# A two-layer hybrid backbone on one core: layer 1's input projection split in three and pipelined by tile, queries and keys projected in turns, values behind the first scores

## The chip, the cores and the metric

One core of one Trainium2 chip. The metric is the device time of one execution in microseconds (us); the kernel before has a median of 1917.29 us over three runs (1916.35 to 1918.03).

## What is computed

A stream of 512 latent and 256 context rows of 1024 features goes through two layers. Layer 0 mixes by a gated linear recurrence, layer 1 by attention; each is followed by a mixture of 16 experts, whose weights (12 MB each) are streamed from HBM. The change lies in layer 1's mixer:

```python
def mla_qkv(h, w_in, q_norm, kv_norm, w_uq, w_ukv, cos, sin):
    z = h @ w_in                                   # 1024 -> 384 + 256 + 32
    cq, ckv, kr = z[..., :384], z[..., 384:640], z[..., 640:]
    q = (rmsnorm(cq, q_norm) @ w_uq).reshape(B, L, 16, 96)
    kv = (rmsnorm(ckv, kv_norm) @ w_ukv).reshape(B, L, 16, 64 + 64)
    # q's last 32 and kr are rotated for latent rows (apply_rope);
    # k = 64 of kv beside kr, the same for all heads; v = the other 64
def attend(q, k, v):
    s = einsum('bqhd,bkhd->bhqk', q, k) * 96 ** -0.5
    return einsum('bhqk,bkhd->bqhd', softmax(s), v)
```

512 latent rows are queries; keys and values come from all 768 rows.

## The kernel before, in words

Everything is written out by hand for five engines, which meet at semaphores only. Rows are worked in tiles of 128: TLT = 4 latent tiles, TT = 6 tiles in all. An F32 tensor that has to go through TensorE faster is kept as a high part of type F32R (a copy by ACT, `hi`) and the rest (a subtraction by DVE, `lo`), and a product is then three matmuls: hi x hi, lo x hi, hi x lo. The scores (L935, L936), layer 0's input projection (L590) and both output projections (L650) do this; layer 1's input projection (L845, L846) and the projections of queries (L899) and of keys and values (L880) are F32 matmuls.

**Input projection of layer 1** (PE L845 and L846, in the loop over `step`). After layer 0's experts the stream is read back into `x_b`. For all six tiles ACT squares and sums (`squares`, L998, L999), DVE scales (`normed_tile`, L1283, L1284), PE turns the tile (`turn_tile`, L516 into `turned`), ACT and DVE modulate half of it each (`modulate`, L1008 and L1292) into `hT2`. ACT and DVE do this in `norm(2)`, for six tiles, before anything else. PE projects tile 0, turns tile 2, projects tile 1, turns tiles 3, 4 and 5, and goes on; a latent tile gets 672 columns, a context tile only the last 288. Behind each projection ACT squares the latent (L1228 to L1232), DVE scales it into `cqn` (L1659 to L1663), copies 32 columns to `kraw` and rotates them into `krr` (L1645, L1670), PE turns `cqn` (L516 into `duo`), and DVE writes `cqT` and `ckvT` (L1678, L1681). PE turns tile t's only when DVE has done the `cqT` of t - 1.

**The attention loop** (`Fori` over NG = 4 groups of HG = 4 heads). A projection stage: six times keys and values (`kv_project`, 512 columns, `duo` bank t % 2), each copied by DVE into `ktok` and `V` (L1699 to L1701), turned by PE (`turn_keys`), copied by ACT to `k_hi` (L1237) and subtracted by DVE to `k_lo` (L1706); then four times queries (`q_project`, 384 columns) with a rotation on DVE (L1718, L1645, L1722), turned, `q_hi` (L1242), `q_lo` (L1728). `turned` has one bank for keys and one for queries, so a turning waits for the low part of the one before. A score stage: 16 units u of one head and one query tile. PE computes scores (`scores`, L935, L936, banks 2 * (u % 2) of `wide`), DVE the maximum (L1745), ACT the exponential (L1259), DVE the reciprocal (L1741), POOL scales (L1877), PE turns the probabilities LAG = 3 units later (L516 into `turned`), ACT and DVE copy them to `PT` (L1251, L1753), and every second unit PE multiplies by the values (`values`, L958) into `duo`.

**Around it.** The output projection (`residual_norm` on DVE, L1455 and L1461 for the low parts of weight blocks and rows) is followed by the choice of rows and the experts. DVE opens the ring's other slots for the experts' weights in `choose`; SP's queue issues every weight load in one fixed order (L463), and four of its slots open at the end of the attention loop.

Of the kernel before, what the change touches and what calls it, by code (L numbers as in the profile page):

```python
# [15 lines left out]
ALU = mybir.AluOpType  # L16
# [6 lines left out]
P = 128  # L23
# [21 lines left out]
def build(nc, x, c, ctx, c_ctx, ada_w, ada_b, norm_mix, norm_ffn, norm_final, lru_w_in, lru_conv_w, lru_conv_b,  # L45
# [143 lines left out]
    with ExitStack() as es:  # L189
# [71 lines left out]
        def flat(a, n, w):  # L261
# [8 lines left out]
        sub, (xn2, hT2, cqn, kraw) = phase(("xn2", [P, TT, D], F32), ("hT2", [P, KD, T], F32),  # L270
                                           ("cqn", [P, 2, QL + KVL], F32), ("kraw", [P, 2, ROPE], F32))
# [64 lines left out]
            "s_S", "s_max", "s_exp", "s_pn", "s_ptr", "s_PTd", "s_PTa", "s_av", "s_OT", "s_rs")]  # L336
        s_fin, s_out, s_nf = sem("s_fin"), sem("s_out"), sem("s_nf")
# [60 lines left out]
        W0 = [2 * KD, 3 * KD]  # L398
        L0 = [KD, KD + TT]
# [104 lines left out]
        def _(pe):  # L504
# [315 lines left out]
            hT = stages[2]["hT"]  # L820
            for j in range(3):
                arrived(("mla_in", j))

            def mla_w(k):
                j = [n for n, (a, b) in enumerate(MLA_K) if a <= k < b][0]
                return ring_at(("mla_in", j))[:, (k - MLA_K[j][0]) * MZ:(k - MLA_K[j][0] + 1) * MZ]

            for step in range(TT + 1):
                if step < TT:
                    t = step  # L830
                    if t >= 2:

                        pe.wait_ge(s_cqn, t - 1)
                    else:

                        pe.wait_ge(s_ye[0], E + 1)
                        pe.wait_ge(s_modcol, 6)

                    pe.wait_ge(s_hTa, N0[2] + t + 1)
                    pe.wait_ge(s_hTd, N0[2] + t + 1)  # L840
                    b = 2 * (t % 2)
                    for k in range(KD):
                        lhs = hT[:, k, t * P:(t + 1) * P]
# [27 lines left out]
            with pe.Fori(0, NG) as g:  # L871

                def kv_project(t):


                    if t < 2:
                        pe.wait_ge(s_OT, g * 2 + (t + 1))
                    pe.wait_ge(s_ktok, g * 6 + (t + 1))
                    for k in range(KKV):
                        ins = mm(duo[:, t % 2, :], ckvT[:, k, t * P:(t + 1) * P],  # L880
                                 ring_at(("ukv", k))[:, bass.ds(g * BANK, BANK)], start=k == 0, stop=k == KKV - 1)
                    ins.then_inc(s_kv, 1)
# [10 lines left out]
                def q_project(t):  # L893

                    if t < 2:
                        pe.wait_ge(s_ktok, g * 6 + (t + 7))
                    pe.wait_ge(s_qtok, g * 4 + (t + 1))
                    for k in range(KQ):
                        ins = mm(duo[:, t % 2, 0:HG * QK], cqT[:, k, t * P:(t + 1) * P],  # L899
# [11 lines left out]
                kv_project(0)  # L911
                for t in range(1, TT):
                    kv_project(t)
                    turn_keys(t - 1)
                q_project(0)
                turn_keys(TT - 1)
                for t in range(1, TLT):
                    q_project(t)
                    turn_queries(t - 1)
                turn_queries(TLT - 1)  # L920
# [61 lines left out]
        def _(act):  # L982
# [28 lines left out]

            def norm(s):
                n = stages[s]["n"]
                for step in range(n + 1):
                    if step < n:
                        squares(s, step)
                    if step >= 1:
                        modulate(s, step - 1)
# [200 lines left out]
            norm(2)  # L1219

            for t in range(TT):
# [10 lines left out]
                fn(mx[:, 3, t:t + 1], mx[:, 1, t:t + 1], ACT.Sqrt, bias=eps[:, 0:1], scale=1.0 / KVL).then_inc(s_mzs, 1)  # L1232
            with act.Fori(0, NG) as g:
                for t in range(TT):
                    act.wait_ge(s_ktr, g * 6 + (t + 1))

                    fn(k_hi[:, :, t * P:(t + 1) * P], turned[0:QK, 1, :].rearrange("p (h n) -> p h n", h=HG),  # L1237
                       ACT.Copy).then_inc(s_khi, 1)
                for t in range(TLT):
# [31 lines left out]
        def _(dve):  # L1271
# [23 lines left out]

            def norm(s):
                n = stages[s]["n"]
                for step in range(n + 1):
                    if step < n:
                        normed_tile(s, step)  # L1300
                    if step >= 1:
                        modulate(s, step - 1)
# [331 lines left out]
            norm(2)  # L1634

            def turn_angles(dst, src, n, t):

                x1 = src.rearrange("p n (a h f) -> p n a h f", a=2, h=2)[:, :, :, 0, :]
                x2 = src.rearrange("p n (a h f) -> p n a h f", a=2, h=2)[:, :, :, 1, :]
                o1 = dst.rearrange("p n (a h f) -> p n a h f", a=2, h=2)[:, :, :, 0, :]  # L1640
                o2 = dst.rearrange("p n (a h f) -> p n a h f", a=2, h=2)[:, :, :, 1, :]
                cos, sin = [ropes[:, t, i, :].rearrange("p (a f) -> p a f", a=2).unsqueeze(1).to_broadcast([P, n, 2, FQ]) for i in range(2)]
                tmp = [rtmp[:, j, 0:n * 2 * FQ].rearrange("p (n a f) -> p n a f", n=n, a=2) for j in range(4)]
                for j, (a_, b_) in enumerate(((x1, cos), (x2, sin), (x1, sin), (x2, cos))):
                    ins = v.tensor_tensor(tmp[j], a_, b_, ALU.mult)  # L1645
                return ins, [(o1, tmp[0], tmp[1], ALU.subtract), (o2, tmp[2], tmp[3], ALU.add)]


            dve.wait_ge(s_rope, 16)
            for step in range(TT + 1):  # L1650
                if step < TT:
# [13 lines left out]
                    if t < TLT:  # L1665
                        chain.step(v.tensor_copy(kraw[:, t % 2, :], kr))
                        ins, rest = turn_angles(krr[:, t:t + 1, :], kraw[:, t % 2:t % 2 + 1, :], 1, t)
                        chain.step(ins)
                        for o, a_, b_, op in rest:
                            ins = v.tensor_tensor(o, a_, b_, op)  # L1670
                        ins.then_inc(s_cqn, 1)
# [236 lines left out]
```

## Time and profile before

| | us |
|---|---|
| median of three runs | 1917.29 |
| the profiled execution | 1916.38 |
| its span, first to last instruction | 1914.6 |
| PE busy | 1655.4 (86%) |
| DVE busy | 653.2 (34%) |
| ACT busy | 514.2 (27%) |
| POOL busy | 202.5 (11%) |
| mean DMA rate over the span | 276 GB/s |

PE busy counts a matmul from its start to a modelled end. The profiled execution's time has 1.8 us around its span. The chain of work that ended last is PE for 61% of the span, SP's queue for 20%.

### The profile page before, as it was taken

How to read it: one execution, taken by the hardware profiler on the slowest of the kernel's cores; microseconds unless marked ns; L12 is line 12 of the kernel's file. 1: busy time of each engine (PE TensorE's matmuls, PEld its weight loads, DVE VectorE, ACT ScalarE, POOL GpSimd, SP SyncE). 2: the span in 40 equal slices, each digit the busy share in tenths (PEclk: the TensorE clock that was granted, in tenths of full speed). 3: DMA queues.
4: the chain of work that ended last, by engine and by line, in shares of the span. 5: the costliest groups of instructions: out<-in, count | busy, mean ns of one | idle time of the engine just before them, and what ended most of it. 6: DMA issues, size and time to landing. Idle time of an engine off the chain costs nothing.

```text
span 1914.6 us, 22850 instructions
## 1 busy us (share of the span) xinstructions
PE 1655.4 (86%) x9277; PEld 816.8 (43%) x9277; DVE 653.2 (34%) x1359; ACT 514.2 (27%) x873; POOL 202.5 (11%) x199
## 2 busy tenths in 40 slices
PE   5999969579999999999879989988849978777874
PEld 2677748323333333333245757757613322222221
DVE  4666664611212212122234655655441101011111
ACT  5678763201101111011141534535300000000001
POOL 1000010000000000000000413413000100000000
PEclk8999989789999999999979899899969999999998
DMA  9454441899999999998741000002589999999997
GB/s 364 165 199 157 176 176 78 338 374 409 410 396 403 404 390 406 382 403 322 254 169 66 1 0 0 0 0 119 209 338 405 398 398 414 400 413 398 412 408 290
DMA packets 92084, 528.61 MB, mean 276 GB/s; under 512 B 11875, under 2 KB 20176, under 8 KB 36448
## 3 DMA queue, kind: packets, MB, share of 16 engines
q1 hardware_dynamic: 80704, 489.84, 63.6%
q0 software_dynamic: 11296, 37.58, 6.9%
q8 instruction: 62, 1.02, 0.2%
q14 instruction: 22, 0.18, 0.0%
HBM read 504.21 MB, written 23.17 MB: 275 GB/s over the span
## 4 chain that ended last, share of the span: by engine, by line
PE 61%; SPq 20%; ACT 6%; DVE 5%; DMA 5%; issue 3%; ACTq 0%; DVEq 0%; POOLq 0%
SPq L463 20%; PE wide L737 14%; PE duo L777 6%; PE wide L650 6%; PE wide L745 6%; PE turned L516 6%; PE wide L590 5%; PE duo L787 3%; PE duo L958 2%; PE wide L935 2%; PE duo L880 2%; DMA sb_ring<-ada_w 2%; DMA sb_ring_x<-moe_w_down 1%; PE duo L899 1%; PE wide L845 1%
## 5 line engine op out<-in xcount | busy, mean ns | idle before, releaser
L737 PE MATMUL wide<-sb_ring_x,sb_xT 128*64 128x512 f32 x1136 | 271.5, 623 | 33.6 <-DMA sb_ring_x<-moe_w_up 32.5
L737 PE MATMUL wide<-sb_ring,sb_xT 128*64 128x512 f32 x912 | 212.3, 607 | 29.1 <-DMA sb_ring<-moe_w_up 27.4
L1565 DVE TENSOR_TENSOR sb_hid<-wide,sb_sg 128x512 f32<-128x512 f32 x32 | 22.1, 692 | 616.6 <-ACT sb_sg L1174 310.9
L1174 ACT ACTIVATE sb_sg<-wide 128x512 f32<-128x512 f32 x32 | 19.2, 599 | 668.2 <-PE wide L745 340.8
L737 PEld LDWEIGHTS wide<-sb_ring_x,sb_xT 128*64 128x64 f32 x1136 | 79.0, 142 | 212.6 <-issue 140.5
L777 PE MATMUL duo<-sb_ring_x,sb_hidT 128*64 128x512 f32 x592 | 138.3, 600 | 10.3 <-DMA sb_ring_x<-moe_w_down 10.1
L1865 POOL DMA_INDIRECT stream<-sb_ye,sb_idx_t x30 | 43.1, 1435 | 901.6 <-DVE sb_ye L1588 901.6
L737 PEld LDWEIGHTS wide<-sb_ring,sb_xT 128*64 128x64 f32 x912 | 62.1, 138 | 166.0 <-issue 108.4
L1877 POOL TENSOR_TENSOR sb_prob<-sb_prob,sb_asum 128x768 f32<-128x768 f32 x64 | 93.9, 1467 | 261.3 <-DVE sb_asum L1741 261.3
L1580 DVE SCALAR_TENSOR_TENSOR sb_ye<-duo,sb_gate_t,sb_gffn 64x512 f32<-64x512 f32 x30 | 22.3, 742 | 203.9 <-PE duo L787 103.6
L1194 ACT ACTIVATE sb_ye<-duo 64x512 f32<-64x512 f32 x30 | 17.9, 596 | 271.1 <-PE duo L787 146.8
L777 PE MATMUL duo<-sb_ring,sb_hidT 128*64 128x512 f32 x368 | 86.1, 600 | 4.9 <-DMA sb_ring<-moe_w_down 4.4
L777 PEld LDWEIGHTS duo<-sb_ring_x,sb_hidT 128*64 128x64 f32 x592 | 38.1, 136 | 97.0 <-issue 67.3
L590 PE MATMUL wide<-sb_hT_hi,sb_w_hi 128*128 128x512 f32 (+1 forms) x256 | 70.2, 355 | 7.7 <-DVE sb_hT_lo L1387 7.7
L1259 ACT ACTIVATE sb_prob<-wide,sb_asum 128x768 f32<-128x768 f32 x64 | 57.9, 904 | 31.6 <-DVE sb_asum L1745 31.6
L590 PE MATMUL wide<-sb_hT_lo,sb_w_hi 128*128 128x512 f32 (+1 forms) x256 | 66.0, 339 | 0.0
L590 PE MATMUL wide<-sb_hT_hi,sb_w_lo 128*128 128x512 f32 (+1 forms) x256 | 65.9, 338 | 0.0
L745 PE MATMUL wide<-sb_ring_x,sb_xT 128*32 128x512 f32 x568 | 65.6, 595 | 0.0
L1745 DVE TENSOR_REDUCE sb_asum<-wide 128x1 f32<-128x768 f32 x64 | 60.7, 948 | 13.2 <-PE wide L936 13.0
L516 PE MATMUL turned<-sb_ident,sb_prob 128*128 128x128 f32 x384 | 54.2, 278 | 5.1 <-ACT sb_PT L1251 5.1
L745 PE MATMUL wide<-sb_ring,sb_xT 128*32 128x512 f32 x456 | 52.7, 595 | 0.0
L1251 ACT ACTIVATE sb_PT<-turned 128x512 f32<-128x512 f32 x64 | 38.1, 596 | 41.8 <-PE turned L516 40.4
(336 smaller groups left out, 2517.4 us busy)
## 6 DMA issues: line engine op xcount, KB each, us to landing
sb_ring_x<-moe_w_up SPq DMA_DIRECT2D x142, 1024.0 KB, 15.0
sb_ring<-moe_w_up SPq DMA_DIRECT2D x114, 1024.0 KB, 18.9
sb_ring_x<-moe_w_down SPq DMA_DIRECT2D x80, 1024.0 KB, 18.0
sb_ring<-moe_w_down SPq DMA_DIRECT2D x48, 1024.0 KB, 16.1
sb_ring<-ada_w SPq DMA_DIRECT2D x40, 1024.0 KB, 6.8
sb_ring<-lru_w_in SPq DMA_DIRECT2D x8, 1024.0 KB, 9.1
sb_ring_x<-ada_w SPq DMA_DIRECT2D x8, 1024.0 KB, 7.5
sb_ring<-lru_w_out SPq DMA_DIRECT2D x4, 1024.0 KB, 6.6
```

Of the source, the lines that this page charges most:

```text
L463: sp.dma_start(dst, src).then_inc(landed[slot], 16)
L516: return nc.tensor.transpose(dst, src, ident[0:n, 0:n])
L590: ins = mm(wide[:, b, :] if i == 0 else wide[:, b + 1, 0:TC], w[:, p % 2, k, :], seg(h[:, k, :], i), start=k == 0 and n == 0, stop=k == KD ...
L650: ins = mm(wide[:, b + n, :], lhs[:, k, :], w[:, n * BANK:(n + 1) * BANK], start=k == 0 and i == 0, stop=k == KD - 1 and i == 2)
L737: ins = mm(wide[n * CAPL:(n + 1) * CAPL, s, :], xT[:, k, 0:CAPL], w[:, at:at + BANK], start=k == 0, stop=k == KD - 1)
L745: ins = mm(wide[n * CAPC:(n + 1) * CAPC, 2, :], xT[:, k, CAPL:M], w[:, n * BANK:(n + 1) * BANK], start=k == 0, stop=k == KD - 1)
L777: ins = mm(lat[n * CAPL:(n + 1) * CAPL, :], hidT[:, 2 * (c % 2) + r, h * CAPL:(h + 1) * CAPL], w[:, r, n * BANK:(n + 1) * BANK], start=c = ...
L787: ins = mm(both[at:at + CAPC, :], hidT_c[:, 2 * (c % 2) + r, h * CAPC:(h + 1) * CAPC], w[:, r, n * BANK:(n + 1) * BANK], start=c == 0, sto ...
L1259: fn(prob[:, u % LAG, :], wide[:, b:b + 2, :].rearrange("p a n -> p (a n)")[:, 0:T], ACT.Exp, bias=asum[:, 0, u % 4:u % 4 + 1], accum_out= ...
L1745: v.tensor_reduce(asum[:, 0, u % 4:u % 4 + 1], wide[:, b:b + 2, :].rearrange("p a n -> p (a n)")[:, 0:T], AX_X, ALU.max, negate=True).then ...
L1865: pool.indirect_dma_start(out=stream, out_offset=bass.IndirectOffsetOnAxis(ap=idx_t[0:M, e:e + 1], axis=0), in_=(ye if e < E - 1 else xg)[ ...
L1877: g_.tensor_tensor(prob[:, u % LAG, :], prob[:, u % LAG, :], asum[:, 2, u % 4:u % 4 + 1].to_broadcast([P, T]), ALU.mult).then_inc(s_pn, 1)
```

## The change

It does four things. (1) Layer 1's input projection becomes three F32R products: ACT copies the eight weight blocks into a new buffer `mla_hi` and each modulated tile into `hT2_hi` (the place of `xn2`), DVE subtracts, in place. (2) The six tiles are pipelined: ACT and DVE prepare three tiles, then one further behind each projection; PE turns tile t + 2 behind projection t. The rotation of `krr` moves from DVE to POOL. (3) In the attention loop queries and keys are projected in turns (`PROJECT`), keys without values (256 columns); the values' projection (256 columns) stands behind the scores of units 0 to 5, with a copy by DVE into `V`; the first multiplication by values waits for all six. (4) In `residual_norm` of both layers DVE subtracts one weight block before the first rows, not two.

```diff
+        sub, (hT2_hi, hT2_lo) = phase(("hT2_hi", [P, TT, D], F32R), ("hT2_lo", [P, KD, T], F32R))
...
+                                                   ("mla_hi", [P, KD, MZ], F32R))
...
+        PROJECT = [("q", 0), ("k", 0), ("q", 1), ("k", 1), ("q", 2), ("k", 2), ("q", 3), ("k", 3), ("k", 4), ("k", 5)]
+        bank_of = {item: i % 2 for i, item in enumerate(PROJECT)}
...
@@ tensor engine, input projection
-                    pe.wait_ge(s_hTa, N0[2] + t + 1)
-                    pe.wait_ge(s_hTd, N0[2] + t + 1)
+                    pe.wait_ge(s_hlo, MLA_L0 + t + 1)
...
-                        if t < TLT:
-                            mm(wide[:, b, 0:QL], lhs, mla_w(k)[:, 0:QL], start=k == 0, stop=k == KD - 1)
-                        ins = mm(wide[:, b + 1, 0:MZ - QL], lhs, mla_w(k)[:, QL:MZ], start=k == 0, stop=k == KD - 1)
+                        if t == 0:
+
+                            pe.wait_ge(s_wlo, MLA_W0 + k + 1)
+                        _, w_hi, w_lo = mla_w(k)
+                        for i, (lhs, w) in enumerate(((lhs_hi, w_hi), (lhs_lo, w_hi), (lhs_hi, w_lo))):
+                            edge = dict(start=k == 0 and i == 0, stop=k == KD - 1 and i == 2)
+                            if t < TLT:
+                                mm(wide[:, b, 0:QL], lhs[:, k, :], w[:, 0:QL], **edge)
+                            ins = mm(wide[:, b + 1, 0:MZ - QL], lhs[:, k, :], w[:, QL:MZ], **edge)
...
-                    for t in {0: (2,), 1: range(3, TT)}.get(step, ()):
-                        turn_tile(2, t)
+                    if step + 2 < TT:
+                        turn_tile(2, step + 2)
@@ tensor engine, loop
+                def v_project(t):
+
+                    if t >= 2:
+
+                        pe.wait_ge(s_V, g * 6 + (t - 1))
+                    for k in range(KKV):
...
+                    ins.then_inc(s_vp, 1)
...
+                for i in range(len(PROJECT) + 1):
+                    if i < len(PROJECT):
+                        what, t = PROJECT[i]
...
+                    if i >= 1:
+                        what, t = PROJECT[i - 1]
+                        if what == "q":
+                            turn_queries(t)
+                        else:
+                            turn_keys(t)
                 pe.wait_ge(s_kT, g * 6 + 7)
...
+                    if w == 0:
+                        pe.wait_ge(s_V, g * 6 + 6)
...
                         scores(u)
+                    if u < TT:
+                        v_project(u)
@@ scalar engine
+            def mla_rows(t):
+
+                modulate(2, t)
+                h, hi, _ = mla_lhs(t)
+                act.wait_ge(s_hTa, N0[2] + t + 1)
+                act.wait_ge(s_hTd, N0[2] + t + 1)
+                fn(hi, h, ACT.Copy).then_inc(s_hhi, 1)
+
+            for t in range(3):
+                squares(2, t)
+                if t >= 1:
+                    mla_rows(t - 1)
...
+                if t + 3 < TT:
+                    squares(2, t + 3)
+                if t + 2 < TT:
+                    mla_rows(t + 2)
@@ vector engine
-                out_weights_lo(lay, 0, 1)
+                out_weights_lo(lay, 0)
                 out_lhs_lo(lay, 0)
-                out_weights_lo(lay, *range(2, KD))
+                out_weights_lo(lay, *range(1, KD))
...
+            def mla_rows(t):
+
+                modulate(2, t)
+                h, hi, lo = mla_lhs(t)
+                dve.wait_ge(s_hhi, MLA_L0 + t + 1)
+                v.tensor_tensor(lo, h, hi.bitcast(F32), ALU.subtract).then_inc(s_hlo, 1)
...
+                        v.tensor_copy(kraw[:, t % 2, :], kr).then_inc(s_cqn, 1)
...
+                    if t + 3 < TT:
+                        normed_tile(2, t + 3)
+                    if t + 2 < TT:
+                        mla_rows(t + 2)
                 if step >= 1:
                     t = step - 1
                     dve.wait_ge(s_cqtr, t + 1)
...
+                    if u < TT:
+
+                        dve.wait_ge(s_vp, g * 6 + (u + 1))
+                        v.tensor_copy(V[:, u, :, :], duo[:, u % 2, 0:HG * VD].rearrange(
+                            "p (h n) -> p h n", h=HG)).then_inc(s_V, 1)
@@ gpsimd
+            for t in range(TLT):
+                pool.wait_ge(s_cqn, t + 1)
+                if t >= 1:
+
+                    pool.wait_ge(s_krr, 6 * t)
+                _, rest = turn_angles(g_, krr[:, t:t + 1, :], kraw[:, t % 2:t % 2 + 1, :], 1, t, s_krr)
+                pool.wait_ge(s_krr, 6 * t + 4)
+                for o, a_, b_, op in rest:
+                    g_.tensor_tensor(o, a_, b_, op).then_inc(s_krr, 1)
```

## Rows read from the trace of the kernel before

**Rows 1.** stretches by stage; window (us), length, busy per engine (instructions), clock, DMA share, GB/s
```profile
967.37:978.98 11.61, 11.61 (x42) 7.90 (x42) 2.89 (x7) 2.58 (x8) 0.00 (x0) 0.85 0.89 347
978.98:988.13 9.15, 9.15 (x36) 6.14 (x35) 2.28 (x6) 2.72 (x7) 0.00 (x0) 1.00 0.00 0
988.13:1000.40 12.27, 4.77 (x31) 3.88 (x30) 8.25 (x30) 8.40 (x27) 0.00 (x0) 0.77 0.00 1
1035.05:1062.14 27.09, 24.61 (x89) 13.20 (x89) 16.48 (x55) 5.35 (x9) 0.00 (x0) 0.94 0.13 51
1062.14:1109.17 47.03, 45.59 (x387) 39.28 (x384) 24.09 (x50) 26.82 (x50) 23.46 (x16) 0.89 0.00 1
1109.17:1134.56 25.39, 22.91 (x90) 12.61 (x89) 17.16 (x56) 5.35 (x9) 0.00 (x0) 1.00 0.00 0
1134.56:1180.26 45.70, 41.97 (x387) 35.75 (x385) 23.66 (x50) 26.60 (x50) 23.47 (x16) 1.00 0.00 0
1400.00:1900.00 500.00, 398.89 (x1732) 125.18 (x1732) 64.27 (x137) 28.70 (x48) 38.28 (x33) 0.95 0.99 392
```

**Rows 2.** timeline of DVE, score stage of the loop's second iteration; start, length, group
```profile
1142.28 0.16 DVE L1741 RECIPROCAL sb_asum<-sb_asum 128x1 f32<-128x1 f32 x1 [1.06 <-ACT sb_prob L1259]
...
1144.44 0.16 DVE L1741 RECIPROCAL sb_asum<-sb_asum 128x1 f32<-128x1 f32 x1 [0.81 <-ACT sb_prob L1259]
```

**Rows 3.** instructions of one line: ns min/median/max, first and last start, shape
```profile
L1135 ACT ACTIVATE sb_OT_hi<-sb_OT x4: 1042/1061/1064, 1324.7 to 1352.3; 128x1024 fp32r<-128x1024 f32 x4
...
L1461 DVE TENSOR_TENSOR sb_OT_lo<-sb_OT,sb_OT_hi x4: 1217/1218/1221, 1326.9 to 1354.7; 128x1024 fp32r<-128x1024 f32 x4
```

**Rows 4.** timeline of PE, scores at full clock (PEld is a weight load)
```profile
1075.98 0.39 PE L935 MATMUL wide<-sb_k_lo,sb_q_hi 96*128 96x512 f32 x1
...
1076.21 0.28 PE L936 MATMUL wide<-sb_k_lo,sb_q_hi 96*128 96x256 f32 x1
...
1076.33 0.40 PE L935 MATMUL wide<-sb_k_hi,sb_q_lo 96*128 96x512 f32 x1
1076.33 0.19 PEld L936 LDWEIGHTS wide<-sb_k_hi,sb_q_lo 96*128 96x128 f32 x1
...
1076.69 0.82 PE L516 MATMUL turned<-sb_ident,sb_prob 128*128 128x128 f32 x6
```

**Rows 5.** timeline of PE, input projection
```profile
988.13 1.04 PE L516 MATMUL turned<-sb_ident,sb_xn 128*128 128x128 f32 x8
...
1026.97 4.05 PE L846 MATMUL wide<-sb_ring,sb_hT 128*128 128x288 f32 x16
```

**Rows 6.** timeline of DVE and ACT, one modulation and the work behind one projection
```profile
994.66 1.37 DVE L1292 TENSOR_SCALAR sb_hT<-turned,sb_cols 128x128 f32<-128x128 f32 x4 [0.75 <-PE turned L516]
...
1021.33 0.49 ACT L1228 ACTIVATE sb_cqn<-wide 128x384 f32<-128x384 f32 x1 [8.12 <-PE wide L846]
...
1022.83 0.16 DVE L1659 RECIPROCAL sb_lam<-sb_mx 128x1 f32<-128x1 f32 x1 [6.17 <-ACT sb_mx L1232]
...
1024.02 0.18 DVE L1666 COPY sb_kraw<-wide 128x32 f32<-128x32 f32 x1
...
1025.65 0.60 DVE L1681 TENSOR_SCALAR sb_ckvT<-duo,sb_pB 128x128 f32<-128x128 f32 x2
```

**Rows 7.** timeline, queries in the projection stage of the loop's second iteration
```profile
1129.38 0.60 PE L516 MATMUL turned<-sb_ident,sb_qtok 128*96 128x128 f32 x4
...
1129.81 2.10 PE L899 MATMUL duo<-sb_ring,sb_cqT 128*128 x6
...
1132.11 0.42 DVE L1718 COPY sb_qtok<-duo 128x256 f32<-128x256 f32 x1 [0.44 <-PE duo L899]
...
1132.47 0.59 ACT L1242 ACTIVATE sb_q_hi<-turned 96x512 fp32r<-96x512 f32 x1 [1.86 <-PE turned L516]
...
1133.37 0.68 DVE L1728 SCALAR_TENSOR_TENSOR sb_q_lo<-turned,sb_q_hi 96x512 fp32r<-96x512 f32 x1
```

**Rows 8.** timeline of PE, start of layer 1's output projection
```profile
1328.23 0.70 PE L650 MATMUL wide<-sb_wo_a,sb_OT_hi 128*128 128x512 f32 x2 [3.17 <-DVE sb_OT_lo L1461]
```

More of the change, by code:

```diff
@@ L819, in _ @@
             turn_tile(2, 1)
[L820 to L826, printed above, removed]
             for step in range(TT + 1):
@@ L909, in turn_queries @@
                     ins.then_inc(s_qtr, 1)
[L911 to L920, printed above, removed]
+                for i in range(len(PROJECT) + 1):
+                    if i < len(PROJECT):
+                        what, t = PROJECT[i]
+                        if what == "q":
+                            q_project(t)
+                        else:
+                            k_project(t)
+                    if i >= 1:
+                        what, t = PROJECT[i - 1]
+                        if what == "q":
+                            turn_queries(t)
+                        else:
+                            turn_keys(t)
                 pe.wait_ge(s_kT, g * 6 + 7)
@@ L1010, in modulate @@
                 ins.then_inc(s_hTa, 1)
[L1012 to L1018, printed above, removed]
             act.wait_ge(s_const, NCONST)
@@ L1218, in _ @@
             act.wait_ge(s_modev, 6)
-            norm(2)
+            for k in range(KD):
+                w, hi, _ = mla_w(k)
+                slot, n, _ = place["mla_in", [j for j, (a, b) in enumerate(MLA_K) if a <= k < b][0]]
+                act.wait_ge(landed[slot], 16 * n)
+                fn(hi, w, ACT.Copy).then_inc(s_whi, 1)
+            def mla_rows(t):
[8 more added lines that the diff above has]
+                    mla_rows(t - 1)
             for t in range(TT):
@@ L1232, in _ @@
                 fn(mx[:, 3, t:t + 1], mx[:, 1, t:t + 1], ACT.Sqrt, bias=eps[:, 0:1], scale=1.0 / KVL).then_inc(s_mzs, 1)
+                if t + 3 < TT:
+                    squares(2, t + 3)
+                if t + 2 < TT:
+                    mla_rows(t + 2)
             with act.Fori(0, NG) as g:
[L1234 to L1239, printed above, removed]
+                for what, t in PROJECT:
+                    if what == "k":
+                        act.wait_ge(s_ktr, g * 6 + (t + 1))
+                        fn(k_hi[:, :, t * P:(t + 1) * P], turned[0:QK, 1, :].rearrange("p (h n) -> p h n", h=HG),
+                           ACT.Copy).then_inc(s_khi, 1)
+                        continue
                     act.wait_ge(s_qtr, g * 4 + (t + 1))
@@ L1294, in modulate @@
                 ins.then_inc(s_hTd, 1)
[L1296 to L1302, printed above, removed]
             def ada_read(i):
@@ L1632, in _ @@
             mod_columns(5)
[L1634 to L1649, printed above, removed]
+            for k in range(KD):
+                w, hi, lo = mla_w(k)
+                dve.wait_ge(s_whi, MLA_W0 + k + 1)
+                v.tensor_tensor(lo, w, hi.bitcast(F32), ALU.subtract).then_inc(s_wlo, 1)
+            def mla_rows(t):
[3 more added lines that the diff above has]
+                v.tensor_tensor(lo, h, hi.bitcast(F32), ALU.subtract).then_inc(s_hlo, 1)
+            for t in range(3):
+                normed_tile(2, t)
+                if t >= 1:
+                    mla_rows(t - 1)
             for step in range(TT + 1):
@@ new lines, in _ @@
+                for i in range(len(PROJECT) + 1):
+                    if i < len(PROJECT):
+                        what, t = PROJECT[i]
+                        if what == "q":
+                            q_tile(t)
+                        else:
+                            k_tile(t)
+                    if i >= 1:
+                        what, t = PROJECT[i - 1]
+                        if what == "q":
+                            q_rest(t)
+                        else:
+                            k_rest(t)
```

134 lines of the change are left out of this document (79 added, 55 removed).

## The prediction

> **What bounds the kernel now.** I read the stretches by stage first, since the change touches one passage: layer 1's input projection (967.4 to 1035.0 us) and the attention loop of four iterations (1035.0 to 1323.8 us). After it, 500 us have the DMA engines 0.99 busy at 392 GB/s [rows 1]: the experts' weights stream, and the stream opens only when the attention is over, so what the attention gives back moves the end one for one; nothing in the stream itself changes.
>
> The PE timeline shows two things in the input projection. A latent tile costs PE 9.15 us, in F32. And between the second and the third tile lie 12.27 us in which PE is busy 4.77 and its granted clock falls to 0.77 of full [rows 1]: PE turns tiles 2 to 5 one after another, each behind ACT's and DVE's modulation, and then waits for the first normalized latent, because ACT and DVE do all six normalizations before they look at the first projection.
>
> In the loop a projection stage takes 25.39 us, 22.91 of it with PE busy, and a score stage 45.70 us at full clock. In the first iteration they took 27.09 and 47.03, at granted clocks of 0.94 and 0.89 [rows 1]; the third iteration repeats the 47.03. In the score stage's first units PE is not the bound: reciprocal follows reciprocal by 2.16 us [rows 2], DVE's maximum and ACT's exponential taking turns.
>
> **The input projection.** *Start, +1.5 us.* The first matmul now needs a copy (1.06) and a subtraction (1.22) of the 1024-wide tile [rows 3] behind the modulation; 0.8 of it lies beside PE's turning of the second tile, so I take 1.5: 968.85 for 967.37. The eight weight copies on ACT and subtractions on DVE (two thirds as wide, so 0.7 and 0.8 us each, 6 us per engine) fit between the end of layer 0's experts and the arrival of the stream rows, where both engines wait; were that cover gone they would cost up to 6.
>
> *A tile, 7.45 us.* Three F32R products take the place of one F32 product. At full clock 512 columns pass in 0.23 us and 256 in 0.12, each with a weight load of its own beside it [rows 4]; 384 and 288 then take 0.175 and 0.135, and 24 such pairs 7.45 us, for 9.15. A context tile is 24 x 0.135 = 3.25, for 3.9 [rows 5]. Bounds: 7.2 if the loads cost nothing, and, with the 0.19 us of a load's record [rows 4] added to each matmul, 16.5. I stay near the low end because the 256-column row already has a load in its 0.12.
>
> *Order.* In series on PE from 968.85: four latent tiles 29.8, 1.5 for the first one's half clock (the first tile took 1.45 longer than the second [rows 1, 5]), four turned tiles of 1.04 [rows 5], three turned latents of 0.6, one context tile 3.25: 1009.4. DVE and ACT need some 9.2 us per tile (squares and roots 1.5, normalization 1.35, cqT 1.4, modulation 1.37 [rows 6], copy, subtraction), against PE's 9.1, with two tiles of lead: they keep up, just. **What is late next** is DVE's FIFO at the end: the sum for tile 5 stands ahead of cqT(2), and PE's fourth turning needs cqT(2). Projection 3 ends near 1004.5; 1.5 + 1.35 + 1.37 + 1.06 + 1.22 + 1.4 and the handings-over put cqT(2) at 1012.6, so PE waits 3 us. Then 0.6, the last tile 3.25, and the tail as before (4.2 us from the last projection to the loop): the loop begins at 1020.8 instead of 1035.05. **-14.2 us.** The rotation of krr leaves DVE (0.65 us per tile off it) for POOL, which has nothing else then; POOL has no row of such small operations, so from 0.2 to 1.5 us each, six a tile: at most 9 us against 9 us per tile, and DVE waits for it only two tiles later and before the loop.
>
> **The loop, projection stage.** Walked with the rows: q takes PE 1.94 and a turning 0.43; the copy starts 0.36 after the projection, DVE's q tile takes 1.26, ACT's copy 0.59, the subtraction 0.68 [rows 7]. Keys alone are 512 columns in place of 1024, so 0.88 by the ratio to q's 1152. In turns, a pair costs q 1.94 + 0.2 + DVE 1.3 + turning 0.43 + handing over = 3.93: k's projection and turning hide inside DVE's 1.3, PE waits 0.6. First turning at 3.5, fourth at 15.3. Then keys 3, 4 and 5 are bound by their chain (turning 0.43, ACT 0.59, DVE 0.69, three handings-over: 2.04 each), and now the scores wait for the last key's low part, which the queries used to cover: scores at 22.7. The same walk of the old order gives 25.2 (measured 25.39 [rows 1]). **-2.5 each.**
>
> **Score stage.** Six projections of values, 0.88 each, come onto PE, and six copies (0.42) onto DVE. Units 0 to 2 have no probabilities to turn: 1.06 (three pairs [rows 4]) + 0.88 fits in 2.16, so they cost nothing while that 2.16 stands. In units 3 to 5 PE has 1.06 + 0.88 + 0.70 for the six turnings [rows 4] = 2.64 for 2.16: +0.48 three times. The copies lie beside ACT's exponential. POOL queue and SP queue issue nothing new. **+1.5 each**, so an iteration is 1.0 shorter, **-4.0** for four.
>
> **The clock.** Before, passages at half clock (1.2 for 2.4 GHz) cost 1.7 at the loop's start and 1.33 in two of four score stages (47.03 for 45.70 [rows 1]), 4.4 in all; the granted 0.89 over 47.03 makes each of the two some 10 us long. The new tail has PE busy 0.9 of 4.8 us ahead of every score stage. The place to compare is ahead of the loop, where PE rested 4.2 us but for a short turning and then ran its first matmuls slow [rows 1, 5]; so I expect a short half-clock passage in all four, and now it hurts more, for the values fill the slack: about 1.6 each, plus 1.3 at the start: 7.7, **+3.3**. Bounds: no fall at all (-4.4), and 10 us of half clock each time, which by the same walk costs 5.1 each, **+17.3**.
> The Trainium skill (TensorE: Matmul & The Clock Gate, Part 1) says that the throttled state is the default and that activity releases it; the fall before the loop agrees, and by it busier first units should end the passage sooner.
>
> **Both output projections.** DVE subtracts weight block 0, then the first rows, then block 1. PE waited 3.17 us for the rows' low part [rows 8]; block 1's subtraction, of the same shape as the rows' (1.22 [rows 3]), stood in it; layer 0 has the same pattern. **-1.1 twice**; block 1 arrives before PE has done block 0's six matmuls.
>
> **Sum**: -14.2 - 4.0 + 3.3 - 2.2 = -17.1. The profiled execution took 1916.38 us, 0.9 under the median of 1917.29; so 1899.3 against it and **1900.2** as a median.
>
> **Rivals.**
> 1. *Long half-clock passages.* 10 us in every score stage: -20.4 + 17.3 = -3.1, 1914; in half of them, 1907. For it: two of four were that long before [rows 1]. Against: PE then had slack, and will not.
> 2. *No falls*: -20.4 - 4.4 + 1.3 = -23.5, 1893.8. For it: iterations two and four had none.
> 3. *F32R pays less.* A tile at 8.3 and 4.0 gives back 4 us: 1904 to 1905; at F32's own time 8 us, 1908.
> 4. *Slower: the weight loads stand in line.* The input projection goes from 80 matmul-and-load pairs to 240. If each new load cost PE 0.087 us or more that nothing hides, the 17.1 and the 3.8 that make a difference are eaten; at the record's 0.19 it is +45.6 less 17.1: 1946. Against it: a 256-column product with its load passes in 0.12 [rows 4].
> The Trainium skill (TensorE: Matmul & The Clock Gate, "LDWEIGHTS" and "Back-to-back issue gap") gives a load columns/1.2 ns, 107 ns for 128, and a spacing set by load and product together; added whole, my estimate from it is 240 x 0.107 = +25.7, 1925.9. The 0.12 us row speaks against taking it whole.
> 5. *Nothing to gain*: the idle 12.27 us only moves, because DVE's FIFO makes PE wait at every tile instead of once. DVE and PE are within 0.1 us per tile; if each of the four steps waited 3 us, -5: 1912.
>
> **How the numbers follow.** Forecast case 0.57, long passages 0.15, no falls 0.12, F32R dearer 0.08, waits at each tile 0.05, slower 0.03. 0.2% is 3.8 us, about what a measurement of this kernel can tell from no change. Cases 1 (all four long) and 5 reach into it with about 0.04. The range goes from 1892 (no falls, tile at 7.2) to 1909 (half of the passages long, or F32R without gain); above it lie all-long, every-tile waits and slower, 0.1 together.
>
> **What would show it.** First loop matmul near 1021 with a latent tile near 7.5 us and no stall over 1.5 us before the last two tiles; one wait of about 3 us ahead of the fourth turned latent. Loop iterations of 70 to 73 us, projection stages of 22.7 with the last wait on k_lo, score stages of 47 to 49 with granted clock below 1.00 in their first 4 us. PE's first output matmul waiting 2 us for OT_lo, not 3.2. Wrong if projection stages are over 24 us, or if a stage after 1300 us changes its length by more than 2 us.

## The result, and the profile of the changed kernel

The changed kernel has a median of 1910.56 us over seven runs (1905.94 to 1915.26), the kernel before 1917.44 beside it (1916.35 to 1919.11): a ratio of 0.9967, with a 95% interval from 0.9954 to 0.9980. A second set of twelve runs gave 0.9970 (0.9958 to 0.9982). So it is faster by 0.3%, some 6 us, where 17 were forecast: 1910.56 lies above the predicted range of 1892 to 1909. The profiled execution took 1912.11 us (its span 1910.4), for a forecast of 1899.3.

First the stretches of the changed kernel (window, length, busy time of each engine with its instructions, granted clock, share and rate of the DMA engines), to be laid beside [rows 1]:

```profile
969.93:980.62 10.69, 10.69 (x56) 10.69 (x57) 3.31 (x7) 2.90 (x8) 0.00 (x0) 0.75 0.82 327
980.62:989.43 8.81, 8.81 (x64) 8.81 (x63) 4.75 (x12) 5.73 (x17) 1.65 (x6) 1.00 0.00 1
...
1024.36:1050.34 25.98, 21.48 (x89) 13.89 (x89) 14.72 (x50) 5.93 (x10) 0.00 (x0) 0.89 0.12 46
1050.34:1099.04 48.70, 47.42 (x408) 41.32 (x408) 25.27 (x55) 26.07 (x49) 23.48 (x16) 0.96 0.01 1
1099.04:1123.00 23.96, 18.74 (x90) 12.51 (x89) 15.32 (x51) 5.93 (x10) 0.00 (x0) 0.98 0.00 0
1123.00:1172.83 49.83, 48.55 (x408) 42.24 (x409) 25.30 (x55) 26.06 (x49) 23.48 (x16) 0.94 0.00 0
1172.83:1196.79 23.96, 18.74 (x91) 12.51 (x89) 15.33 (x51) 5.93 (x10) 0.00 (x0) 1.00 0.00 0
1196.79:1245.51 48.72, 47.44 (x409) 41.31 (x409) 25.18 (x55) 26.07 (x49) 23.48 (x16) 0.96 0.00 0
1245.51:1269.46 23.95, 18.74 (x90) 12.51 (x89) 15.33 (x51) 5.93 (x10) 0.00 (x0) 0.99 0.00 0
1269.46:1319.44 49.98, 48.70 (x408) 42.35 (x408) 25.41 (x55) 26.67 (x50) 23.48 (x16) 0.94 0.00 0
```

Two things are to be seen. The loop begins at 1024.36 where it began at 1035.05, so the input projection gave what it was made for. But the loop takes 295.1 us where it took 288.7: its projection stages are shorter (23.96 for 25.39), its score stages longer (48.7 to 50.0 for 45.7 to 47.0), and the clock is under 1.00 in all four score stages. So 10.7 us are won ahead of the loop and 6.4 given back in it.

Where the input projection ends, the timeline of PE in the changed kernel (start, length, group, idle time before it and what ended that):

```profile
1013.91 1.30 PE L551 MATMUL duo<-sb_ident,sb_cqn 128*128 128x128 f32 x5 [3.42 <-DVE sb_ckvT L1743]
...
1015.24 0.44 PE L878 MATMUL wide<-sb_mla_hi,sb_hT_lo 128*128 128x288 f32 x1
1015.48 0.44 PE L878 MATMUL wide<-sb_ring_r,sb_hT_hi 128*128 128x288 f32 x1
...
1019.76 0.29 PE L878 MATMUL wide<-sb_ring_r,sb_hT_hi 128*128 128x288 f32 x1
1019.89 0.29 PE L878 MATMUL wide<-sb_mla_hi,sb_hT_hi 128*128 128x288 f32 x1
...
1024.36 1.00 PE L945 MATMUL duo<-sb_ring,sb_cqT 128*128 x1 [1.19 <-DVE sb_marks L1345]
```

The forecast wait for cqT(2) is there, 3.42 us of it. Behind it the matmuls of the last tile start 0.24 us apart, and 0.13 apart from 1019.76 on: two levels of the clock, read off the starts.

A stretch of the second iteration's projection stage, PE and DVE, in the changed kernel:

```profile
1102.84 0.64 PE L551 MATMUL turned<-sb_ident,sb_qtok 128*96 128x128 f32 x4 [0.73 <-DVE sb_qtok L1776]
...
1105.26 0.60 PE L551 MATMUL turned<-sb_ident,sb_ktok 128*96 128x128 f32 x4
1105.54 0.42 DVE L1772 COPY sb_qtok<-duo 128x256 f32<-128x256 f32 x1 [0.71 <-PE duo L945]
...
1106.53 0.36 DVE L1776 TENSOR_TENSOR sb_qtok<-sb_rtmp 128x64 f32<-128x64 f32 x2
...
1107.02 0.64 PE L551 MATMUL turned<-sb_ident,sb_qtok 128*96 128x128 f32 x4 [0.30 <-DVE sb_qtok L1776]
...
1118.80 0.61 PE L551 MATMUL turned<-sb_ident,sb_ktok 128*96 128x128 f32 x4 [0.63 <-DVE sb_k_lo L1782]
...
1120.91 0.61 PE L551 MATMUL turned<-sb_ident,sb_ktok 128*96 128x128 f32 x4 [1.49 <-DVE sb_k_lo L1782]
...
1123.00 0.79 PE L984 MATMUL wide<-sb_k_hi,sb_q_hi 96*128 96x512 f32 x1 [1.48 <-DVE sb_k_lo L1782]
```

A pair of query and key takes 4.18 us from turning to turning. Then the last three keys go one behind another, 2.1 us each, and PE rests 0.63, 1.49 and 1.48 us between short turnings. The first score product behind that takes 0.79 us; the same product has 0.48 at full clock (keys_then_queries, in the last section). At the loop's end the output projection waits as forecast, 2.08 us, 1.1 less than in [rows 8]:

```profile
1322.83 0.70 PE L685 MATMUL wide<-sb_wo_a,sb_OT_hi 128*128 128x512 f32 x2 [2.08 <-DVE sb_OT_lo L1520]
```

### The profile page after: what moved, and what is told of

Read it like the earlier page. It is cut to its first block and busy times, and to the rows that moved or that the text cites. A ratio compares the mean times of both kernels' runs of the same rounds, so it can differ in the third digit from the quotient of the medians.

```text
span 1910.4 us, 23222 instructions
## 1 busy us (share of the span) xinstructions
PE 1649.8 (86%) x9453; PEld 843.8 (44%) x9453; DVE 662.3 (35%) x1349; ACT 524.7 (27%) x887; POOL 208.7 (11%) x223
## 3 DMA queue, kind: packets, MB, share of 16 engines
q8 instruction: 63, 1.03, 0.2%
```

## The experiments

All times are medians, each with its ratio to the kernel before run on the same chip. The theory after the result: the loop half of the change loses by itself, because turning in series leaves the last keys' chain bare, and because PE's rest ahead of the scores lets the clock fall.

### The two halves apart

*input_only* has parts (1), (2) and (4) of the change with the old loop; *loop_only* has part (3) with everything else as before. The cut shows one place of input_only's edit.

```diff
 # input_only: PE, ACT and DVE in the loop as before
-                for i in range(len(PROJECT) + 1):
...
+                kv_project(0)
+                for t in range(1, TT):
+                    kv_project(t)
+                    turn_keys(t - 1)
```

> The changed input projection and output order with the old attention loop. Theory (the loop is what lost: its projection stages gain 1.4 us each, its score stages lose 3 us each, half of that to a clock that falls ahead of each): the loop begins near 1024.4 as in the changed kernel, takes some 288.7 us as before, and the time is 11 to 14 us under the kernel before, 1903 to 1906. Rival (the loop is neutral and the 13 us won in the input projection are lost again behind the loop, at the expert weights): the same 1910 as the whole change.

> The old input projection and output order with the changed attention loop. Theory: the loop takes 294 to 296 us where it took 288.7, so the kernel is 5 to 7 us slower than the kernel before, 1922 to 1924. The prediction's own sum had the loop shorter by 0.7 us in all: 1916 to 1917. Rival (the loop's loss comes only from its earlier start or from what the new input projection leaves behind, such as the rotated columns): no slower than the kernel before.

Measured: input_only 1905.00 (0.9940, 0.9927 to 0.9953), its loop beginning at 1021.77 and taking 288.7 us; loop_only 1924.56 (1.0039, 1.0025 to 1.0053), 0.6 above its range. The second iteration of loop_only:

```profile
1111.27:1135.23 23.96, 18.74 (x91) 12.52 (x89) 15.32 (x51) 5.93 (x10) 0.00 (x0) 1.00 0.00 0
1135.23:1183.95 48.72, 47.44 (x408) 41.28 (x408) 25.18 (x55) 26.07 (x49) 23.47 (x16) 0.96 0.00 0
```

They equal the third iteration of the whole change, and the loop as a whole takes 294.5 us for its 295.1: the loop's loss has nothing to do with what stands ahead of it. The halves add up: -0.60% and +0.39%, together -0.21% for -0.33% and -0.30% measured, within the intervals. Nothing that could be told from the scatter was lost behind the loop; the change is a gain of some 12 us and a loss of some 7.

### The clock

*fill* puts useless products where PE rests; *fill_last*, made later, keeps the one directly ahead of the scores.

```diff
+                def fill():
+                    pe.wait_ge(s_ktok, g * 6 + 7)
+                    for k in range(KKV):
+                        ...
+                        mm(duo[:, 0, 0:HG * VD], ckvT[:, k, 0:P], w, start=k == 0, stop=k == KKV - 1)
...
                         else:
+                            if t >= 4:          # fill only
+                                fill()
                             turn_keys(t)
+                fill()
                 pe.wait_ge(s_kT, g * 6 + 7)
```

> The changed kernel with useless products of two matmuls each (256 columns, F32, the shape of the values' projection) at three places where PE waits for the last keys: ahead of the turnings of keys 4 and 5 and ahead of the scores. PE does the same work otherwise. Theory (PE's rest ahead of the scores lets the clock fall, and the fall costs some 2 us a score stage): granted clock 0.99 or more in all score stages, score stages 46.5 to 47.5 instead of 48.7 to 50.0, projection stages within 0.5 us of 23.96, and the time 5 to 9 us under the changed kernel, 1902 to 1906. Rival (the clock is a bystander, the score stages are long because the values' projections collide with units 3 to 5): score stages stay at 48.5 or more, time 1910 or more.

> The changed kernel with the useless product at one of the three places only, directly ahead of the scores; the rests ahead of the turnings of keys 4 and 5 stay. Theory A (what counts is PE's rest directly ahead of the scores): score stages near 47.2 at granted clock 1.00 as with all three, time 1900 to 1904. Theory B (it is the whole tail, some 4.8 us in which PE does little, that lets the clock fall): the fall stays in at least two of four score stages, 47.9 to 50, time 1904 to 1911.

Measured: fill 1901.38 (0.9908, 0.9893 to 0.9922; 0.6 under its range), fill_last 1901.21 (0.9915, 0.9898 to 0.9932). The second iteration of fill, then of fill_last:

```profile
1096.34:1120.41 24.07, 21.21 (x102) 14.60 (x101) 15.32 (x51) 5.92 (x10) 0.00 (x0) 1.00 0.00 0
1120.41:1167.61 47.20, 45.92 (x409) 40.18 (x409) 25.08 (x55) 26.05 (x49) 23.46 (x16) 1.00 0.00 0
```
```profile
1096.22:1120.19 23.97, 19.61 (x95) 13.18 (x93) 15.33 (x51) 5.93 (x10) 0.00 (x0) 1.00 0.00 0
1120.19:1167.29 47.10, 45.82 (x409) 40.08 (x409) 25.11 (x55) 26.07 (x49) 23.48 (x16) 1.00 0.00 0
```

PE does more work and the kernel is 9 us faster (11.6 between fill_last and the changed kernel on one chip; in the profiles fill's loop takes 8 us less). In fill the score stages are at full clock, 47.1 to 47.2 us in all four iterations, so a fall cost 1.5 us in the first and third and 2.6 to 2.8 in the second and fourth. The 47.2 is also the clean price of the values' projections: 1.5 over the 45.70 of [rows 1]. One product directly ahead of the scores gives nearly what three give, but not all of it. In the third iteration of fill_last the clock fell once more, before that product: the turning behind the rest of 1.50 us took 1.06 us instead of 0.61, the product 1.91 instead of 1.03. The cost was 0.4 us in the projection stage and 0.2 to 0.3 in the scores. The third iteration's two stages, then the product in the second iteration beside the third's:

```profile
1167.29:1191.70 24.41, 20.67 (x95) 13.98 (x93) 15.32 (x51) 5.93 (x10) 0.00 (x0) 0.94 0.00 0
1191.70:1239.09 47.39, 46.11 (x410) 40.31 (x409) 25.11 (x55) 26.07 (x49) 23.48 (x16) 0.99 0.00 0
```
```profile
1118.54 1.03 PE L934 MATMUL duo<-sb_ring,sb_ckvT 128*128 x4
...
1189.15 1.06 PE L551 MATMUL turned<-sb_ident,sb_ktok 128*96 128x128 f32 x4 [1.50 <-DVE sb_k_lo L1790]
1190.00 1.91 PE L934 MATMUL duo<-sb_ring,sb_ckvT 128*128 x4
```

So neither theory of fill_last holds whole: the rests ahead of the last two turnings brought a fall by themselves once in four iterations, and the last rest is what made it come in every one.

### The same values in the idle places

*values_tail* puts real work there: values 0 to 3, with 4 and 5 behind scores 0 and 1.

```diff
+                            if t == 4:
+                                v_project(0)
+                            if t == 5:
+                                v_project(1)
+                                v_project(2)
                             turn_keys(t)
+                v_project(3)
                 pe.wait_ge(s_kT, g * 6 + 7)
...
-                    if u < TT:
-                        v_project(u)
+                    if u < 2:
+                        v_project(u + 4)
```

> The changed kernel with the values' projections 0 to 3 moved out of the score stage into the same idle places (one ahead of the turning of keys 4, two ahead of keys 5, one ahead of the scores), 4 and 5 behind the scores of units 0 and 1. Theory: the clock stays at full, projection stages stay at 24 to 24.5 since 0.88 us of product fits in each 1.5 us of rest, score stages return to 45.7 to 46.2, an iteration takes 70 and the time is 1895 to 1899. Rival (values cost the same wherever they stand, or DVE's four copies delay the low parts of the keys): projection stages of 25.5 or more, time 1903 or more.

Measured: 1896.59 (0.9885, 0.9871 to 0.9900).

```profile
1096.61:1120.74 24.13, 21.90 (x107) 15.43 (x105) 16.64 (x55) 5.92 (x10) 0.00 (x0) 1.00 0.00 0
1120.74:1166.27 45.53, 43.47 (x392) 37.33 (x392) 23.90 (x52) 25.93 (x49) 23.46 (x16) 1.00 0.00 0
```

PE is busy 3.2 us more in the projection stage than in the changed kernel, and the stage is only 0.2 longer: that much of it was idle. The score stage is back at 45.5, the time it has without any values: two projections behind units 0 and 1 cost nothing, as the prediction said of the units that have no probabilities to turn.

### Which half of the loop change pays

*turns_values_in* has queries and keys in turns, with the values still projected with the keys; *keys_then_queries* has the values behind the scores, but keys first and queries last, as before. In its order P is a projection and T its turning; DVE's order and the waits for a free bank follow it.

```diff
 # turns_values_in
+                        w = ring_at(("ukv", k))[:, bass.ds(g * BANK, BANK)]
+                        ins = mm(duo[:, bank_of["k", t], :], ckvT[:, k, t * P:(t + 1) * P], w, start=k == 0, stop=k == KKV - 1)
-                    if u < TT:
-                        v_project(u)
 # keys_then_queries
-        PROJECT = [("q", 0), ("k", 0), ("q", 1), ("k", 1), ("q", 2), ("k", 2), ("q", 3), ("k", 3), ("k", 4), ("k", 5)]
+        PE_ORDER = """Pk0 Pk1 Tk0 Pk2 Tk1 Pk3 Tk2 Pk4 Tk3 Pk5 Tk4 Pq0
+                    Tk5 Pq1 Tq0 Pq2 Tq1 Pq3 Tq2 Tq3""".split()
```

> The changed kernel with only one half of its loop change: queries and keys in turns, but values projected with the keys (512 columns) and copied by DVE with them, as before; nothing behind the scores. Theory (walked with the durations of the changed kernel's trace: turning in series leaves the last keys' chain uncovered, and that costs more than turns give): projection stages of 26.2 to 26.8 us, longer than the 25.39 before, so turns alone are a loss; score stages 45.7 to 48; the time 1906 to 1911. Rival (turns are what shortens the projection stage, as the prediction's credit of 2.5 us a stage reads): projection stages under 25.4.

> The other half: values projected behind the first scores as in the changed kernel, but all keys first and then all queries, the order of the kernel before. Theory: the queries cover the last keys' chain, so projection stages are 22.7 to 23.1 us against 23.96 in turns, PE rests less ahead of the scores, the score stages are 47.2 to 48.5 against 48.7 to 50.0, and the time is 1898 to 1905, 5 to 12 us under the changed kernel with less code changed. Rival (turns help): projection stages at 24 or more and a time of 1910 or more.

Measured, with input_only and the changed kernel in the table's other corners (all four have the new input projection):

| | values with the keys | values behind the scores |
|---|---|---|
| keys, then queries | 1905.00; stage 25.40 | **1897.12** (0.9894, 0.9879 to 0.9909); stage 22.64 |
| in turns | 1910.33 (0.9958, 0.9944 to 0.9971); stage 25.93 | 1910.56; stage 23.96 |

The second iteration of turns_values_in, then of keys_then_queries:

```profile
1098.91:1124.84 25.93, 22.95 (x91) 12.80 (x89) 17.88 (x57) 5.93 (x10) 0.00 (x0) 0.99 0.00 0
1124.84:1171.81 46.97, 45.54 (x384) 39.15 (x385) 23.30 (x49) 26.11 (x49) 23.48 (x16) 0.90 0.00 0
```
```profile
1097.36:1120.00 22.64, 18.45 (x91) 12.37 (x89) 14.74 (x50) 5.33 (x9) 0.00 (x0) 1.00 0.00 0
1120.00:1167.12 47.12, 45.84 (x411) 40.07 (x408) 25.69 (x56) 26.65 (x50) 23.46 (x16) 1.00 0.00 0
```

Moving the values is the whole gain of the loop change, 8 us, and only in the old order. In turns it gives nothing (1910.33 and 1910.56): what the projection stages save, the score stages give back. Turns lose in either column, 13 to 14 us in the right one and 4 to 5 in the left, where the 95% intervals still overlap and the loops of the two profiles differ by 3.7 us. They make the projection stage longer (0.5 and 1.3 us) and leave PE waiting for k_lo right ahead of the scores. With queries last, the last key's low part is ready long before PE is through, and only the last turning waits; in keys_then_queries the clock fell in the first score stage alone (48.7 us, the other three 47.1 to 47.2). The walk had put turns_values_in at 26.2 to 26.8 a stage, at least 0.3 too dear; the time of keys_then_queries lies 0.9 under its range.

### The wait ahead of the fourth turned latent

*latent_first* moves one step in DVE's queue.

```diff
             def mla_rows(t):
                 modulate(2, t)
+                if t >= 3:
+                    latent_turned(t - 3)     # cqT and ckvT, with its wait for s_cqtr
                 h, hi, lo = mla_lhs(t)
                 dve.wait_ge(s_hhi, MLA_L0 + t + 1)
```

> The changed kernel with one step of DVE's queue moved: in the input projection the transposed latent of tile t - 3 (cqT) is scaled behind the modulation of tile t, while ACT makes the high part, and ahead of the low part, instead of behind it. Theory (the wait of 3.42 us ahead of the fourth turned latent is DVE's queue order, and the half clock of the last context tile comes from that rest): the wait is under 1.5 us, the last context tile takes 3.2 to 3.3 us instead of 5.4, the loop begins at 1020 to 1021.5 instead of 1024.4, and the time is 3 to 4 us under the changed kernel, 1906 to 1908. Rival (the low part of tile 5 becomes what PE waits for, by as much): loop begins at 1023.5 or later.

Measured: 1906.86 (0.9941, 0.9927 to 0.9954); the loop begins at 1020.17.

```profile
1011.71 0.74 PE L551 MATMUL duo<-sb_ident,sb_cqn 128*128 128x128 f32 x5 [1.00 <-DVE sb_ckvT L1705]
1012.84 0.37 PE L878 MATMUL wide<-sb_mla_hi,sb_hT_hi 128*128 128x288 f32 x1 [0.39 <-DVE sb_hT_lo L1716]
1016.10 0.38 PE L551 MATMUL duo<-sb_ident,sb_cqn 128*128 128x128 f32 x2
```

The wait is 1.00 and 0.39 us for 3.42, and the last tile 3.26 us for 5.43 at half clock. Of the 4.2 us, half is the wait and half the half clock behind it. That second half is there only in executions in which the clock falls, which they don't all do (the input projection, below).

### A version that beats both, and the changed kernel again

*mixed_order* takes its order from a walk of PE, ACT and DVE with the durations of the changed kernel's trace; *mixed_latent_first* adds the step above.

```diff
+        PE_ORDER = """Pk0 Pk1 Pk2 Tk0 Pq0 Tk1 Pq1 Pk3 Tk2 Tq0 Pk4 Pk5
+                    Tk3 Pq2 Tq1 Tk4 Pq3 Tq2 Tk5 Pv0 Pv1 Tq3 Pv2""".split()
+        DVE_ORDER = """Ck0 Ck1 Rk0 Ck2 Cq0 Rk1 Cq1 Ck3 Rk2 Ck4 Rq0 Rk3
+                    Ck5 Cq2 Rq1 Rk4 Cq3 Rq2 Cv0 Rk5 Cv1 Rq3""".split()
```

P is a projection, T its turning, C the copy out of `duo` (for queries with the rotation), R the low part, k, q and v are keys, queries and values; the copy of value 2 and values 3 to 5 stand behind the first scores.

> A version made from the findings: the projection stage in an order found by walking PE, ACT and DVE with the durations of the changed kernel's trace (keys 0 to 2 first, queries 0 and 1, keys 3 to 5, queries 2 and 3, values 0 to 2 where the last keys and queries are under way, values 3 to 5 behind scores 0 to 2). Theory (the stage is then bound by PE's own 20.2 us of work, PE never rests ahead of the scores and the clock stays): projection stages 20.2 to 20.8 us, score stages 45.6 to 46.2, an iteration 66 to 67, and the time 1880 to 1885. Rival (a wait that the walk doesn't show, on DVE's queue above all): iterations of 68.5 or more and a time of 1890 or more.

> The mixed order of the projection stage together with the latent ahead of the low part. Theory (two places that don't touch: the gains add): the loop begins at 1019 to 1021, iterations of 65.8, the output projection begins near 1287.5, and the time is 3 to 4 us under the mixed order alone (1880.0), 1875 to 1878. Rival (beyond the loop the expert weights arrive no earlier, so nothing is won any more): 1880 or more.

> The changed kernel itself once more, beside the two next ones on one chip. Expected: a median of 1909 to 1912 and, if the wide scatter of its first seven times (1905.9 to 1915.3) belongs to the kernel and is no accident, a scatter of more than 4 us again; projection stages 23.95, score stages between 48.7 and 50.2.

Measured: mixed_order 1880.02 (0.9803, 0.9789 to 0.9816), mixed_latent_first 1875.52 (0.9776, 0.9760 to 0.9792), 41.5 us under the kernel before. Two stretches of mixed_order:

```profile
1090.54:1110.65 20.11, 20.11 (x103) 15.12 (x101) 15.31 (x52) 5.49 (x10) 0.00 (x0) 1.00 0.00 0
1110.65:1156.26 45.61, 44.00 (x399) 38.11 (x397) 25.08 (x54) 26.16 (x50) 23.46 (x16) 1.00 0.00 0
```

PE is busy in every microsecond of the projection stage; an iteration takes 65.7 us for 72.7 to 73.8. The changed kernel again gave 1912.81 (1902.74 to 1915.70), 0.8 above its range. Its profiled execution is its fastest, 1902.74, and has the same loop, falls included, within 0.6 us (one score stage, in the fence below). It was short elsewhere: layer 1's rows were turned from 961.0 on for 963.9, from there to the loop it took 57.2 us for 60.5, and 584.9 us lay behind the start of the output projection for 587.6. So the difference of these two executions isn't the loop's. The kernel before scatters too in that set, if less: 1915.47 to 1923.20.

```profile
1043.57:1093.41 49.84, 48.56 (x408) 42.24 (x409) 25.30 (x55) 26.06 (x49) 23.48 (x16) 0.94 0.01 1
```

## Why the prediction was wrong, step by step

The forecast of 1899.3 for the profiled execution was 12.8 us too low. By its own terms:

**The projection stages, 4.3 us: the step that failed.** The walk in turns gave 22.7 us and the sum 22.9 (25.39 less 2.5); the stages took 23.96. A pair came to 3.93 for 4.18 measured, three times, by four small terms: it let DVE's copy start 0.2 us after the projection where its own reading of [rows 7] was 0.36 (0.28 measured, 1105.26 to 1105.54), and took 0.43 for a turning (0.48), 1.3 for DVE's part (1.35, 1105.54 to 1106.89) and 0.06 for the handing over (0.13). The first turning came 0.3 later (3.8 for 3.5), the tail's three keys 2.10 each for 2.04. None of these is large; together they are 1.2 us a stage, half of the 2.5 credited. What the sum didn't ask was what the same walk gives with the old order: it said 22.7 to 23.1 when it was asked, and 22.64 was measured. The prediction took the two ideas of the loop change as one and credited the pair with what only one of them earns.

**The clock, 2.7 us.** Right in kind: a short fall ahead of all four score stages, as the tail suggested. Too cheap: 1.6 each was taken, 1.5 and 2.6 to 2.8 measured (8.4 for 6.4), and the first projection stage had 2.0 over the clean one, for 1.3. Rival 1 feared passages of 10 us; they were shorter than before. With u the length of a passage at half clock, 0.96 over 48.70 us is u = 3.9 us and 0.94 over 49.83 is 6.0, where 0.89 over 47.03 [rows 1] was 10.3. The Trainium skill (TensorE: Matmul & The Clock Gate, Part 1) lets activity release the throttle; these rows agree, the busier first units have the shorter passages.

**Values behind the scores, right.** +1.5 was forecast, 1.5 measured at full clock.

**The input projection, 3.6 us.** The loop began at 1024.36 for 1020.8. The F32R tiles are right: 24 pairs from 980.62 to the turning at 988.10 take 7.48 us, against 7.45. The wait for cqT(2) is right too (3.4 for 3). Missed: the first matmul came 1.1 late (969.93 for 968.85, 0.9 of it there at the first turning already), the first tile took 2.4 longer than the second for 1.5, and 2.5 us that the fourth turned latent and the last tile had more at half clock (0.95 for 0.6, 5.43 for 3.25). Against that, the turnings between the tiles took 4.8 us for the 6.0 summed. The half clock stands behind the forecast wait: the sum held a rest of 3 us and a full clock right behind it, though [rows 1] showed the clock down after PE's rests. But it isn't bound to come. Nine profiled executions have this wait of 3.4 us; in seven the turning behind it took 1.30 us, in two it took 0.74 and the last tile ran at full clock. The two are the second profile of the changed kernel (first fence) and input_only (second):

```profile
1010.30 0.74 PE L551 MATMUL duo<-sb_ident,sb_cqn 128*128 128x128 f32 x5 [3.42 <-DVE sb_ckvT L1743]
...
1014.08 0.38 PE L551 MATMUL duo<-sb_ident,sb_cqn 128*128 128x128 f32 x2
```
```profile
1013.83 0.74 PE L551 MATMUL duo<-sb_ident,sb_cqn 128*128 128x128 f32 x5 [3.41 <-DVE sb_ckvT L1721]
```

So 2.5 of the 12.8 us belong to the execution that was profiled, not to the kernel alone; what decides between the two cases is open.

**The weight loads, rival 4, are out.** 240 matmuls with a load each in place of 80 pass at the price that the sum took from [rows 4], 7.48 us for the 24 pairs of a tile. The Trainium skill (TensorE: Matmul & The Clock Gate, "LDWEIGHTS") would have added 25.7 us by my estimate if nothing were hidden; the trace shows them hidden.

**The output projections.** -1.1 in layer 1 is there [rows 8]. In layer 0 it is there too, by PE's group with its idle time, 13.1 us in the kernel before, and in the changed one:

```profile
L685 PE MATMUL wide<-sb_wo_a,sb_ring_r 128*128 128x512 f32 x36 | 12.9, 441 | 12.1 <-DVE sb_Y_lo L1520 12.1
```

That is 1.0 us less, but the first turning of layer 1's rows came at 963.9 for 963.0. That instant lay between 961.0 and 964.8 over all the profiled executions, so what became of 1 us can't be read; it counts as 1.1 against the sum. The stretch from the output projection to the end took 1.2 us more, within its scatter (584.9 to 588.8 in all but one of the profiled executions).

In all: 4.3 + 2.7 + 3.6 + 1.1 + 1.2 = 12.9.

**The time and the chances.** 0.93 for faster holds, if barely: 0.30% to 0.33% against a bound of 0.2%. Neither of its two signs of being wrong came: the projection stages of 23.96 lie just under its 24 us, and what lies behind the loop, taken as a whole, changed by 1.2 us for the 2 allowed. The first sign had been set too far out to catch the step that failed. The range was too tight above. It was made of rivals taken one at a time, while several terms, all on the dear side, came together.

## What to carry to other kernels

When a change joins two ideas in one loop, walk each alone with the same durations before crediting the pair: here one was worth 8 us and the other cost 4 to 14, and the same walk could have told. In a software pipeline ask what covers the last item's chain; a filler with independent work (queries, values) belongs at the end, not spread through the middle. And wherever a sum contains a rest of TensorE, give the work behind that rest two prices, at full and at half clock, or put real work into the rest: that was worth 8 to 9 us here even with useless work.

## What was not expected of the hardware

- With queries and keys in turns PE rests 1.48 us directly ahead of the scores, behind a short turning and a rest of 1.49, and the clock fell just ahead of the scores or at their start in every iteration, twenty of twenty in five profiles. A product of 0.88 us in that place alone kept it up in three iterations of four. With queries last PE also rests 1.76 us shortly ahead of the scores, but behind a long projection (below, keys_then_queries): there the clock fell in one score stage of four, and in two of four in the kernel before and in input_only, which end their projection stage in the same way. So behind the same pattern of work and rest the clock falls in one iteration and not in the next.

```profile
1115.25 2.10 PE L951 MATMUL duo<-sb_ring,sb_cqT 128*128 x6
1117.26 0.61 PE L557 MATMUL turned<-sb_ident,sb_qtok 128*96 128x128 f32 x4
1119.63 0.61 PE L557 MATMUL turned<-sb_ident,sb_qtok 128*96 128x128 f32 x4 [1.76 <-DVE sb_q_lo L1792]
1120.00 0.48 PE L987 MATMUL wide<-sb_k_hi,sb_q_hi 96*128 96x512 f32 x1
```

- The falls in the changed kernel alternate, 1.5 and 2.6 to 2.8 us, in the first profile, in the second (score stages of 49.8, 48.7, 50.0 and 48.8) and in loop_only; in latent_first they are less regular (49.3, 50.1, 48.7, 50.2). Why is open.
- POOL's (GpSimd's) small operations cost little: 0.32 us for a product of 128x16 and 0.22 for a sum, so the rotation took 1.7 us a tile, near the low end of the 1.2 to 9 that was allowed for (groups of the changed kernel: busy, mean ns).

```profile
L424 POOL TENSOR_TENSOR sb_rtmp<-sb_kraw,sb_ropes 128x16 f32<-128x16 f32 x16 | 4.7, 322 | 38.8 <-DVE sb_kraw L1729 38.8
L1962 POOL TENSOR_TENSOR sb_krr<-sb_rtmp 128x16 f32<-128x16 f32 x8 | 1.6, 222 | 0.3
```
